# One weighted sum of squares for two norms, and one block from the feed-forward's output to the second projection

## The chip, the cores and the metric

The kernel runs on one core of a Trainium2 chip. A core has a matrix engine (TensorE, PE in the profile), two elementwise engines (VectorE, DVE; ScalarE, ACT), a slower general one (GpSimd, POOL) and SyncE (SP), which here only issues DMAs. The engines run side by side and wait for each other by semaphores. The metric is the device time of one launch in microseconds (us); lower is better.

## The reference, cut to what matters

The program is two transformer blocks over 256 tokens of width 1024, in float32. The place of the change is the end of the first block and the beginning of the second:

```python
# end of the first block
    hn = rms_norm(h, norm_ffn)
    gate_ffn, up_ffn = jnp.split(hn @ w_ffn_in, [FFN_HIDDEN], axis=-1)
    h = h + (jax.nn.silu(gate_ffn) * up_ffn) @ w_ffn_out
    x = rms_norm(h, norm_final)                  # the stream of the second block
# begin of the second block
    ada = silu(c) @ w_ada + b_ada                # gives shift and scale vectors
    xn = rms_norm_2(x, norm1_w) * (1 + scale) + shift
    proj = xn @ w_in                             # 4104 columns: qkv, gates, and beta and decay (8 columns)
    ...                                          # x itself is needed again for the residual
```

`rms_norm(x, g)` is `x * rsqrt(mean(x*x) + 1e-6) * g`. The feed-forward's hidden width is 2816. The three `ada` lines are written here in short; only the two vectors matter.

## The kernel before, in words

The activations lie transposed: 1024 channels are 8 groups (`KD`) of 128 partitions, and 256 tokens (`T2`) run along the free dimension. Every matrix product is done as three fast matmuls: an operand is split into a high part (an ACT copy to the matmul's format, "hi") and the rest (a DVE subtraction, "lo"), and hi·hi, hi·lo and lo·hi are added up in PSUM. So each weight tile costs an ACT copy and a DVE subtraction before PE can use it; three buffers of each (`CUT`) let that run ahead. A few small products are done with plain float32 operands; the profile shows each such matmul as two rows. Weights come by SP's DMA queue into a ring of three slots of 2 MB (`load_slots`, L221).

The stretch in question is a chain of program blocks. A block ends with all engines meeting.

1. **The feed-forward's block** (from L1587). PE makes 22 pairs of gate and up tiles (L1595). The norm before it is applied late: DVE scales the gate by `frs` (L1647), ACT takes the sigmoid (L1630), DVE multiplies gate and sigmoid (L1651) and then by up (L1653); the factor that is still missing is put on the output. Then 11 pieces of output weights (L1610) add into 8 PSUM banks. In each piece the two hidden groups are taken one after the other over all 8 banks. At the end DVE scales each bank by `frs2` (L1663) and adds it to the stream `hT` (L1665).
2. **`rms_norm`** (L236 to L261): squares on DVE and ACT, 8 float32 matmuls with a matrix of ones to sum them (L248), a square root on ACT (L254), a reciprocal (L259) and 8 scalings on DVE (L261). It is the first block's final norm.
3. **A block** in which ACT copies the normed stream to `xT` (L1680) and DVE and ACT compute a few columns of gains and bounds (L1687 to L1709).
4. **`rms_norm` again**, now the second block's first norm, with a shift added by ACT (L269).
5. **A block** with one GpSimd memset (L1723).
6. **`project`** (L294) for the second projection, with 32 tiles of 128 columns. ACT and DVE first split the activations as a whole and three weight tiles (L332, L351). Then PE does one tile after the other (24 matmuls each, L385), ACT and DVE empty the banks in turn (L1728, L1729), split the weights three tiles ahead, and do in hooks (`front_pe`, `front_act`, `front_dve`) what the finished tiles allow: the short convolution (L1829, L1832), its activation (L1803, L1837), squares and their sums (L1840, L1778). After tile 1 PE also makes the 8 columns of beta and decay with 16 float32 matmuls (L1769). DVE makes 4 copies at tile 30 (L1862).

Nothing here is scheduled by a tool. The order on every engine is the order in which the code is written.

## Time and profile before

| | us |
|---|---|
| median of 3 runs (lowest to highest) | 1763.94 (1761.31 to 1767.03) |
| the profiled execution, whole | 1757.34 |
| its span, first to last instruction | 1755.6 |
| PE busy in the span | 1536.9 (88%) |
| DVE busy | 1009.0 (57%) |
| ACT busy | 675.2 (38%) |
| POOL busy | 140.3 (8%) |

The page gives busy time per engine, 40 slices of the span, and the costliest groups of instructions by source line. The finer views are the timeline (one row for an instruction or for several alike, with its start, its duration, and in brackets how long the engine had been idle and who released it) and the table by stretches (busy time of every engine in given windows and the clock granted to PE, where 1.00 is 2.4 GHz and 0.50 is 1.2 GHz). PE's matmuls overlap: one is shown as 0.28 us long, but at full clock one starts every 0.12 us.

### The profile page before, as it was taken

Reading aid. Unit: us, or ns where it says so; the run is one execution under the profiler, and the core shown is the slowest. Engines: PE = TensorE matmul, PEld = TensorE weight load, DVE = VectorE, ACT = ScalarE, POOL = GpSimd, SP = SyncE. Lnnn points to the kernel's source line nnn. Section 1 sums busy time; section 2 is a strip of 40 time slices with the busy share of each in tenths; the row PEclk is TensorE's granted clock in tenths of the full one; section 3 lists DMA queues with packets and bytes.
Section 4 is the critical chain, followed back from the end, with each engine's and each line's share of the span. In section 5 each row is a group of like instructions: output and inputs, shape, how many; then the busy total and the mean of one; then the engine's idle time right before and its main releaser. Section 6 shows DMA issues by size and latency. Waiting matters only on the chain. (4 is left out here: it accounts for less than half of the span.)

```text
span 1755.6 us, 29260 instructions
## 1 busy us (share of the span) xinstructions
PE 1536.9 (88%) x11916; PEld 1278.5 (73%) x11916; DVE 1009.0 (57%) x1501; ACT 675.2 (38%) x910; POOL 140.3 (8%) x238
## 2 busy tenths in 40 slices
PE   7987697999999679976466679999999999999996
PEld 6975485999999659946456677777777777777774
DVE  5546565486664448544484555656566665566653
ACT  4342324455443244511413433444444444444441
POOL 7000000000000000000040020000000000000000
PEclk9976798999999889979687789999999999999998
DMA  7422300545554517350050386988988899988880
GB/s 250 156 96 88 106 4 1 192 155 188 190 190 142 122 48 155 134 192 1 26 167 1 119 303 250 346 331 323 344 320 337 330 335 333 341 333 337 333 314 24
DMA packets 113221, 349.27 MB, mean 199 GB/s; under 512 B 9633, under 2 KB 33392, under 8 KB 96448
## 3 DMA queue, kind: packets, MB, share of 16 engines
q1 hardware_dynamic: 103184, 315.75, 50.3%
q0 software_dynamic: 8240, 27.40, 5.2%
q10 hardware_dynamic: 1664, 4.26, 0.7%
q8 instruction: 94, 1.54, 0.4%
q14 instruction: 39, 0.32, 0.1%
HBM read 345.15 MB, written 2.23 MB: 198 GB/s over the span
## 5 line engine op out<-in xcount | busy, mean ns | idle before, releaser
L2830 DVE TENSOR_TENSOR weights_lo<-raw_weights,weights_hi 128x2048 fp32r<-128x2048 f32 x99 | 223.8, 2288 | 82.7 <-ACT weights_hi L2734 82.7
L2734 ACT ACTIVATE weights_hi<-raw_weights 128x2048 fp32r<-128x2048 f32 x99 | 185.4, 1910 | 23.4 <-DMA raw_weights<-in_w_gate 20.0
L2536 PE MATMUL bank<-x_hi,weights_hi 128*128 128x256 f32 x544 | 154.8, 285 | 0.0
L2537 PE MATMUL bank<-x_lo,weights_hi 128*128 128x256 f32 x544 | 154.6, 284 | 0.0
L2538 PE MATMUL bank<-x_hi,weights_lo 128*128 128x256 f32 x544 | 154.6, 284 | 0.0
L385 PE MATMUL bank<-in_x_hi,in_w_hi 128*128 128x256 f32 (+2 forms) x472 | 139.3, 295 | 15.9 <-DVE in_w_lo L351 15.9
L385 PE MATMUL bank<-in_x_hi,in_w_lo 128*128 128x256 f32 (+2 forms) x472 | 137.3, 291 | 0.0
L385 PE MATMUL bank<-in_x_lo,in_w_hi 128*128 128x256 f32 (+2 forms) x472 | 137.2, 291 | 0.0
L2616 PE MATMUL bank<-raw_weights,gathered_pair 128*64 128x512 f32 x512 | 113.4, 595 | 0.0
L2536 PEld LDWEIGHTS bank<-x_hi,weights_hi 128*128 128x128 f32 x544 | 105.1, 193 | 2.3 <-issue 1.6
L1508 DVE TENSOR_TENSOR ffn_weights_lo<-weight_ring,ffn_weights_hi 128x2048 fp32r<-128x2048 f32 x33 | 75.6, 2293 | 54.0 <-ACT ffn_weights_hi L1503 54.0
L2537 PEld LDWEIGHTS bank<-x_lo,weights_hi 128*128 128x128 f32 x544 | 105.2, 193 | 0.7
L2538 PEld LDWEIGHTS bank<-x_hi,weights_lo 128*128 128x128 f32 x544 | 105.1, 193 | 0.0
L351 DVE TENSOR_TENSOR in_w_lo<-weight_ring,in_w_hi 128x1024 fp32r<-128x1024 f32 (+1 forms) x59 | 71.5, 1217 | 58.5 <-ACT in_w_hi L332 58.5
L385 PEld LDWEIGHTS bank<-in_x_hi,in_w_hi 128*128 128x128 f32 (+1 forms) x472 | 91.8, 194 | 17.8 <-DVE in_w_lo L351 16.4
L1595 PE MATMUL bank<-merge_x_hi,ffn_weights_hi 128*128 128x256 f32 x352 | 99.3, 282 | 2.6 <-PEq L319 2.6
L1595 PE MATMUL bank<-merge_x_lo,ffn_weights_hi 128*128 128x256 f32 x352 | 99.1, 281 | 0.0
L1595 PE MATMUL bank<-merge_x_hi,ffn_weights_lo 128*128 128x256 f32 x352 | 99.0, 281 | 0.0
L385 PEld LDWEIGHTS bank<-in_x_lo,in_w_hi 128*128 128x128 f32 (+1 forms) x472 | 91.9, 195 | 0.3
L385 PEld LDWEIGHTS bank<-in_x_hi,in_w_lo 128*128 128x128 f32 (+1 forms) x472 | 91.7, 194 | 0.1
L385 PE MATMUL bank<-merge_x_hi,merge_w_hi 128*128 128x256 f32 x256 | 73.8, 288 | 11.7 <-DVE merge_w_lo L351 9.8
L2616 PEld LDWEIGHTS bank<-raw_weights,gathered_pair 128*64 128x64 f32 x512 | 35.3, 137 | 66.6 <-issue 66.6
(579 smaller groups left out, 3749.3 us busy)
## 6 DMA issues: line engine op xcount, KB each, us to landing
raw_weights<-in_w_gate SPq DMA_DIRECT2D x64, 1024.0 KB, 8.8
raw_weights<-in_w_up SPq DMA_DIRECT2D x64, 1024.0 KB, 9.0
raw_weights<-in_w_down SPq DMA_DIRECT2D x64, 1024.0 KB, 8.4
weight_ring<-in_w_in SPq DMA_DIRECT2D x17, 2048.0 KB, 9.1
mixer_memory<-in_w_ada SPq DMA_DIRECT2D x96, 256.0 KB, 3.8
weight_ring<-in_w_ffn_in SPq DMA_DIRECT2D x22, 1024.0 KB, 6.7
weight_ring<-in_w_ffn_out SPq DMA_DIRECT2D x5, 2048.0 KB, 7.9
weight_ring<-in_w_out SPq DMA_DIRECT2D x4, 2048.0 KB, 7.7
```

The source lines that it names most:

```text
L351: s_tlo.on(V.tensor_tensor(lo, src, hi.bitcast(F32), ALU.subtract))
L385: mm = T.matmul(bank[m % banks][0:w, 0:n], weights[:, k, :], x[:, r0 + k, :], start=(k == 0 and weights is hi and x is x_hi), stop=(k == r ...
L1508: s_rest.on(V.tensor_tensor(as_piece(f_lo[r % CUT], r), src, as_piece(f_hi[r % CUT], r).bitcast(F32), ALU.subtract))
L1595: mm = T.matmul(bank[2 * (m % 4) + up][:, 0:T2], w[:, k, up, :], x[:, k, :], start=(k == 0 and w is hi and x is fx_hi), stop=(k == KD - 1 ...
L2536: T.matmul(out_, hi[:, d, cut], x_hi[:, d, :], start=(d == 0), stop=False)
L2537: T.matmul(out_, hi[:, d, cut], x_lo[:, d, :], start=False, stop=False)
L2538: mm = T.matmul(out_, lo[:, d, cut], x_hi[:, d, :], start=False, stop=(d == KD - 1))
L2616: mm = T.matmul(bank[4][lanes, :].rearrange("p (a b) -> p a b", b=FE), xp[:, d, lanes], raw_w[:, r:r + 2, d * FE:d * FE + FE], start=(d == ...
L2734: S.activation(w_hi[:, n % 4, :], raw_w[:, k % RAW, :], ACT.Copy).then_inc(s_hi.sem, 1)
L2830: V.tensor_tensor(w_lo[:, n % 4, :], raw_w[:, k % RAW, :], w_hi[:, n % 4, :].bitcast(F32), ALU.subtract).then_inc(s_lo.sem, 1)
```

## The change

- The two norms become one. With g the final norm's gain, the product of both inverse norms is 1 / sqrt(mean(h² (g² + eps)) + eps²). So one sum of h² weighted by (g² + eps) is enough, and the second block's input is made from `hT` directly. ACT squares with the square root of the weight as scale; GpSimd adds 5 of the 7 further squares into the first (named `second_squares`), the last two go to PE separately: 3 float32 matmuls with ones in place of 8.
- In the feed-forward, up is normed as well (one more DVE operation per pair, `fup`), so that the output needs no scaling: one DVE add per bank in place of a multiplication and an add.
- The last piece of output weights goes bank by bank (both hidden groups of a bank in a row), so that each bank is finished 6 matmuls after the one before.
- The whole stretch from the feed-forward to the end of the projection is one block. The projection's first three weight tiles are split ahead of the norm's work. Its activations are split group by group as they are made (ACT makes hi with the shift, DVE makes lo from the same source), and PE takes tiles 0 and 1 together, group by group.
- The 8 columns of beta and decay use split operands: 48 fast matmuls in place of 16 float32 ones.
- The stream itself (the final norm's output, for the residual) is normed during the projection: 8 ACT squares at tiles 8 to 11, 7 GpSimd adds, one float32 matmul at tile 16, a logarithm and an exponential on ACT at tiles 20 and 25, 8 DVE scalings at tiles 29 and 30. The few columns of gains and bounds move to tiles 19 and 26. `xT` is now a view of `hT`, and its copy is gone.
- Tensors are placed at offsets written out, so that what used to be freed and taken anew can overlap in time.

The core of the diff:

```diff
 def project(..., weights_first=False, together=1):
+                    if together > 1:
+                        source = tiles[0][3]
+                        group = [operands(("w", m)) for m in range(together)]
+                        pe.wait_ge(s_tlo.sem, split_at["w", together - 1])
+                        for k in range(KD):
+                            pe.wait_ge(late[source].sem, late[source].count(k + 1))
+                            for m, (_, hi, lo) in enumerate(group):
+                                for weights, x in ((hi, x_hi), (hi, x_lo), (lo, x_hi)):
+                                    mm = T.matmul(bank[m][...], weights[:, k, :], x[:, k, :], ...)
...
 # feed-forward, DVE, pair m
-                    s_hid.on(V.tensor_tensor(fprod, bank[b], fsig, ALU.mult))
-                    s_hid.on(V.tensor_tensor(fprod, fprod, bank[b + 1], ALU.mult))
+                s_up_n.on(V.tensor_tensor(fup, bank[b + 1], frs, ALU.mult))
+                s_hid.on(V.tensor_tensor(fprod, fgate, fsig, ALU.mult))
+                s_hid.on(V.tensor_tensor(fprod, fprod, fup, ALU.mult))
...
-                for m in range(KD):
-                    s_out_n.on(V.tensor_tensor(fout[:, m % 2, :], bank[m][:, 0:T2], frs2, ALU.mult))
-                    dve_s.on(V.tensor_tensor(hT[:, m, N_META:T1], hT[:, m, N_META:T1], fout[:, m % 2, :], ALU.add))
-        rms_norm(hT[:, :, N_META:T1], x_new, lambda j: param("norm_final", j), None, ...)
-                act_s.on(S.activation(xT, x_new, ACT.Copy))
-        rms_norm(xT, hm, lambda j: gain1[:, j:j + 1], lambda j: mod[:, j:j + 1], ...)
+        def second_norm_dve(dve):
+            for m in range(KD):
+                dve.wait_ge(s_out_m.sem, s_out_m.count(m + 1))
+                s_added.on(V.tensor_tensor(xT[:, m, :], xT[:, m, :], bank[m][:, 0:T2], ALU.add))
+            dve.wait_ge(s_root2.sem, s_root2.count(1))
+            s_root2.on(V.reciprocal(rs_in, rs_in))
+            for m in range(KD + 1):
+                if m < KD:
+                    s_t2.on(V.scalar_tensor_tensor(out=ht[:, m, :], in0=xT[:, m, :], scalar=gain_in[:, m:m + 1], in1=rs_in, ...))
+                if m:
+                    dve.wait_ge(s_x2hi.sem, s_x2hi.count(m))
+                    s_x2lo.on(V.scalar_tensor_tensor(out=x2_lo[:, m - 1, :], in0=ht[:, m - 1, :], scalar=mod[:, m - 1:m], ...))
+        def second_norm_act(act):
+            for m in range(KD):
+                act.wait_ge(s_added.sem, s_added.count(m + 1))
+                s_sq2.on(S.activation(squares2[:, m, :], xT[:, m, :], ACT.Square, scale=gain_root[:, m:m + 1]))
+            act.wait_ge(s_sum2.sem, s_sum2.count(1))
+            s_root2.on(S.activation(rs_in, bank[0][:, 0:T2], ACT.Sqrt, bias=eps_in, scale=1.0 / D))
+            for m in range(KD):
+                act.wait_ge(s_t2.sem, s_t2.count(m + 1))
+                s_x2hi.on(S.activation(x2_hi[:, m, :], ht[:, m, :], ACT.Identity, bias=mod[:, m:m + 1]))
```

The order of instructions shows it at two places. First PE, from the last output matmuls of the feed-forward (bank 7) to the first of the projection. Before:

```order
L1610 MATMUL bank6<-ffn_hidden_hi,ffn_weights_lo2 128x256
L1610 MATMUL bank7<-ffn_hidden_hi,ffn_weights_hi2 128x256
L1610 MATMUL bank7<-ffn_hidden_lo,ffn_weights_hi2 128x256
L1610 MATMUL bank7<-ffn_hidden_hi,ffn_weights_lo2 128x256
L1576 UNCONDITIONAL_BRANCH
L243 UNCONDITIONAL_BRANCH
L248 MATMUL bank0<-mixer2_kept,kept 128x256 x8
L230 UNCONDITIONAL_BRANCH
L243 UNCONDITIONAL_BRANCH
L248 MATMUL bank0<-mixer2_kept,kept 128x256 x8
L230 UNCONDITIONAL_BRANCH
L372 UNCONDITIONAL_BRANCH
```

And in the changed kernel (the numbers behind names only number the tensors):

```order
L1682 MATMUL bank7<-ffn_hidden_hi_5168,ffn_weights_lo2_3842 128x256
L1690 MATMUL bank0<-second_squares_5179,kept 128x256
L1693 MATMUL bank0<-second_squares_5179,kept 128x256 x2
L381 UNCONDITIONAL_BRANCH
L391 MATMUL bank0<-in2_x_hi_5177,in2_w_hi0_5171 128x256
L391 MATMUL bank0<-in2_x_lo_5178,in2_w_hi0_5171 128x256
L391 MATMUL bank0<-in2_x_hi_5177,in2_w_lo0_5174 128x256
L391 MATMUL bank1<-in2_x_hi_5177,in2_w_hi1_5172 128x256
L391 MATMUL bank1<-in2_x_lo_5178,in2_w_hi1_5172 128x256
L391 MATMUL bank1<-in2_x_hi_5177,in2_w_lo1_5175 128x256
```

Sixteen summing matmuls have become three, the meetings of all engines between them are gone (one branch is left), and banks 0 and 1 take turns by group of channels. The second place is DVE between the feed-forward's last bank and the projection's tiles. Before:

```order
L1663 TENSOR_TENSOR ffn_memory<-bank7,ffn_memory 128x256
L1665 TENSOR_TENSOR kept<-kept,ffn_memory 128x256
...
L236 TENSOR_TENSOR mixer2_kept<-kept 128x256 x4
L256 UNCONDITIONAL_BRANCH
L259 RECIPROCAL mixer2_kept<-mixer2_kept 128x256
L261 SCALAR_TENSOR_TENSOR mixer2_kept<-kept,mixer2_kept 128x256 x8
...
L1709 TENSOR_SCALAR kept<-kept 128x4
...
L351 TENSOR_TENSOR in2_x_lo<-mixer2_kept,in2_x_hi 128x2048
L351 TENSOR_TENSOR in2_w_lo0<-weight_ring,in2_w_hi0 128x1024
```

In the changed kernel:

```order
L360 TENSOR_TENSOR in2_w_lo2_5176<-weight_ring,in2_w_hi2_5173 128x1024
L1761 SCALAR_TENSOR_TENSOR kept<-kept 128x8
...
L1773 TENSOR_TENSOR kept<-kept,bank0 128x256
...
L1773 TENSOR_TENSOR kept<-kept,bank7 128x256
L1775 RECIPROCAL ffn_memory_3845<-ffn_memory_3845 128x256
L1779 SCALAR_TENSOR_TENSOR mixer2_kept_5170<-kept,ffn_memory_3845 128x256 x2
L1783 SCALAR_TENSOR_TENSOR in2_x_lo_5178<-mixer2_kept_5170,kept,in2_x_hi_5177 128x256
L1779 SCALAR_TENSOR_TENSOR mixer2_kept_5170<-kept,ffn_memory_3845 128x256
...
L360 TENSOR_TENSOR in2_w_lo0_5174<-weight_ring,in2_w_hi0_5171 128x1024
L1805 COPY mixer2_kept_5170<-bank1 128x256
```

The three weight splits stand ahead of the stream's adds now, one reciprocal is left of two, and scaling and splitting alternate group by group.

## Rows read from the trace of the kernel before

**Rows 1.** Timeline, PE: last output matmul to the third projection tile.
```profile
593.73 0.28 PE L1610 MATMUL bank<-ffn_hidden_hi,ffn_weights_lo 128*128 128x256 f32 x1
598.78 5.13 PE L248 MATMUL bank<-mixer_kept,kept 128*128 128x256 f32 x16 [4.76 <-DVE mixer_kept L236]
614.84 5.63 PE L248 MATMUL bank<-mixer_kept,kept 128*128 128x256 f32 x16 [10.93 <-DVE mixer_kept L236]
632.78 0.58 PE L385 MATMUL bank<-in_x_hi,in_w_hi 128*128 128x256 f32 x1 [12.31 <-DVE in_w_lo L351]
640.04 7.07 PE L1769 MATMUL bank<-mixer_kept,kept 128*4 128x256 f32 x32
647.04 0.39 PE L385 MATMUL bank<-in_x_hi,in_w_hi 128*128 128x256 f32 x1
```

**Rows 2.** Timeline, DVE: the same stretch.
```profile
591.53 0.43 DVE L1663 TENSOR_TENSOR ffn_memory<-bank,ffn_memory 128x256 f32<-128x256 f32 x1 [10.46 <-PE bank L1610]
...
597.55 0.43 DVE L1665 TENSOR_TENSOR kept<-kept,ffn_memory 128x256 f32<-128x256 f32 x1
...
604.46 1.75 DVE L259 RECIPROCAL mixer_kept<-mixer_kept 128x256 f32<-128x256 f32 x1 [4.73 <-ACT mixer_kept L254]
606.24 3.26 DVE L261 SCALAR_TENSOR_TENSOR mixer_kept<-kept,mixer_kept 128x256 f32<-128x256 f32 x8
...
631.51 3.49 DVE L351 TENSOR_TENSOR in_w_lo<-weight_ring,in_w_hi 128x1024 fp32r<-128x1024 f32 x3
```

**Rows 3.** Timeline, ACT: the same stretch.
```profile
603.95 0.47 ACT L254 ACTIVATE mixer_kept<-bank,kept 128x256 f32<-128x256 f32 x1 [3.04 <-PE bank L248]
...
623.33 3.30 ACT L269 ACTIVATE mixer_kept<-mixer_kept,kept 128x256 f32<-128x256 f32 x8 [2.34 <-DVE mixer_kept L261]
```

**Rows 4.** Windows of 2 us: busy time per engine (count), then PEclk, DMA, GB/s.
```profile
596.00:598.00 2.00, 0.00 (x0) 0.00 (x0) 1.91 (x5) 0.00 (x0) 0.00 (x0) 1.00 0.00 0
598.00:600.00 2.00, 1.22 (x3) 1.05 (x4) 1.43 (x4) 1.71 (x5) 0.00 (x0) 0.56 0.00 0
...
634.00:636.00 2.00, 2.00 (x11) 2.00 (x11) 1.00 (x1) 0.00 (x0) 0.00 (x0) 0.55 0.00 0
636.00:638.00 2.00, 2.00 (x19) 2.00 (x18) 0.00 (x0) 0.73 (x2) 0.00 (x0) 1.00 0.00 0
```

**Rows 5.** Timeline, POOL, DVE, ACT: adding squares ahead of the feed-forward.
```profile
391.73 1.07 POOL L1554 TENSOR_TENSOR ffn_memory<-ffn_memory 128x256 f32<-128x256 f32 x1 [1.81 <-ACT ffn_memory L1533]
397.05 0.74 POOL L1554 TENSOR_TENSOR ffn_memory<-ffn_memory 128x256 f32<-128x256 f32 x1 [4.24 <-ACT ffn_memory L1533]
...
392.13 0.96 DVE L1544 SCALAR_TENSOR_TENSOR merge_x_lo<-kept,merge_x_hi 128x256 fp32r<-128x256 f32 x1
...
397.10 0.41 DVE L1519 TENSOR_TENSOR kept<-kept,bank 128x256 f32<-128x256 f32 x1
398.09 0.48 DVE L1544 SCALAR_TENSOR_TENSOR merge_x_lo<-kept,merge_x_hi 128x256 fp32r<-128x256 f32 x1 [0.58 <-ACT merge_x_hi L1532]
...
396.57 0.40 ACT L1533 ACTIVATE ffn_memory<-kept 128x256 f32<-128x256 f32 x1
```

**Rows 6.** Groups by line and shape, PE, 15 to 120 us: a narrow weight tile.
```profile
L385 PE MATMUL bank<-in_x_hi,in_w_hi 128*128 128x272 f32 x208 | 61.7, 296 | 3.6 <-DVE in_w_lo L351 3.6
...
L385 PE MATMUL bank<-in_x_hi,in_w_hi 128*32 128x272 f32 x8 | 2.3, 287 | 0.0
```

**Rows 7.** Timeline, DVE: a late pair of the feed-forward's input.
```profile
522.29 0.42 DVE L1651 TENSOR_TENSOR ffn_memory<-bank,ffn_memory 128x256 f32<-128x256 f32 x1 [0.49 <-ACT ffn_memory L1630]
```

**Rows 8.** Who waited for whom, 632 to 745 us: total, times, longest.
```profile
ACT mixer_kept L1728 <- PE bank L385: 41.6, 11, 11.3
...
PE bank L1778 <- DVE mixer_kept L1840: 2.1, 2, 1.1
```

**Rows 9.** Timeline, DVE: the projection's last tiles.
```profile
742.21 2.48 DVE L1862 COPY mixer_memory<-bank 128x512 f32<-128x512 f32 x4
747.61 0.42 DVE L1729 COPY mixer_kept<-bank 128x256 f32<-128x256 f32 x1 [2.93 <-PE bank L385]
```

More of the change, by code:

```diff
@@ L146, in build @@
         row_sel = mem.take(GH, P)
+        AT_SMALL = mem.at
         small = mem.take(256)
@@ L373, in _ @@
                 def _(pe):
+                    if together > 1:
[6 more added lines that the diff above has]
+                                for weights, x in ((hi, x_hi), (hi, x_lo), (lo, x_hi)):
+                                    mm = T.matmul(bank[m][0:tiles[m][2], 0:n], weights[:, k, :], x[:, k, :],
+                                                  start=(k == 0 and weights is hi and x is x_hi), stop=(k == KD - 1 and weights is lo))
+                                if k == KD - 1:
+                                    pe_s.on(mm)
+                        if "pe" in between:
+                            for m in range(together):
+                                between["pe"](pe, m)
                     for m, (s, c0, w, source) in enumerate(tiles):
+                        if together > 1 and m < together:
+                            continue
                         pe.wait_ge(s_tlo.sem, max(split_at["w", m], split_at.get(("x", source), 0)))
@@ new lines, in _ @@
+        @block.scalar
+        def _(act):
+            for r in range(1, CUT):
+                cut_piece(act, r)
+            act.wait_ge(s_hsum.sem, s_hsum.count(1))
+            s_hlog.on(S.activation(flog, bank[7][:, 0:T2], ACT.Ln, bias=eps_rms, scale=1.0 / D))
+            act.wait_ge(s_hlog.sem, s_hlog.count(1))
+            s_hrs.on(S.activation(frs, flog, ACT.Exp, scale=-0.5))
+            for m in range(n_in):
+                act.wait_ge(s_gate_n.sem, s_gate_n.count(m + 1))
+                if m >= 2:
+                    act.wait_ge(s_hid.sem, s_hid.count(2 * (m - 1)))
+                s_sig.on(S.activation(fsig[:, m % 2, :], fgate[:, m % 2, :], ACT.Sigmoid))
+                cut_piece(act, m + CUT)
+                act.wait_ge(s_hid.sem, s_hid.count(2 * m + 2))
+                s_fhi.on(S.activation(ffn_hi[m], fprod[:, m % 2, :], ACT.Copy))
+            for r in range(n_in + CUT, n_in + n_out):
+                cut_piece(act, r)
@@ L1766, in front_pe @@
             if m == 1:
+                pe.wait_ge(s_bahi.sem, s_bahi.count(2))
                 for i in range(2):
                     for k in range(KD):
[L1769 to L1770 removed]
+                        for w, x in ((ba_hi, x2_hi), (ba_hi, x2_lo), (ba_lo, x2_hi)):
+                            mm = T.matmul(bank[4][0:GH, i * T2:i * T2 + T2], w[:, k, GH * i:GH * i + GH], x[:, k, :],
+                                          start=(k == 0 and w is ba_hi and x is x2_hi), stop=(k == KD - 1 and w is ba_lo))
                 s_ba.on(mm)
@@ L1779, in front_pe @@
                 s_ssq.on(mm)
+            if m == 16:
+                pe.wait_ge(s_stracc.sem, s_stracc.count(KD - 1))
+                s_strn.on(T.matmul(bank[5][:, 0:T2], ones, ht[:, 0, :], start=True, stop=True))
             if m == 28:
+                pe.wait_ge(s_strn.sem, s_strn.count(2))
                 pe.wait_ge(s_row_dve.sem, 4)
@@ L1865, in front_dve @@
                 dve_s.on(V.tensor_copy(cols, bank[6][:, 0:4 * GH].rearrange("p (a b) -> p a b", b=GH)))
-        with ExitStack() as stack:
-            project([hm], T2, [(W_IN2 + m // 4, (m % 4) * P, P, 0) for m in range(32)], put_in2, W_IN2, 8,
-                    split_memory(stack, "in2_", KD, T2), banks=4, between={"pe": front_pe, "act": front_act, "dve": front_dve})
-        MIX2B = total - SECOND - MIX2 - 32
-        m2b = Memory(mixer_stack.enter_context(nc.sbuf_tensor("mixer2_late", [P, MIX2B], F32)), 0, MIX2B)
+        project([None], T2, [(W_IN2 + m // 4, (m % 4) * P, P, 0) for m in range(32)], put_in2, W_IN2, 8,
+                (x2_hi, x2_lo, w2_hi, w2_lo), banks=4, late={0: s_x2lo}, block=block, together=2,
+                between={"pe": front_pe, "act": front_act, "dve": front_dve,
+                         "act_first": second_norm_act, "dve_first": second_norm_dve})
+        ffn_stack.close()
+        MIX2B = AT_MIX2 - AT_PARTS2
+        m2b = Memory(place("mixer2_late", [P, MIX2B], AT_PARTS2, F32), 0, MIX2B)
         Dm = m2b.take(2 * GH, P)
```

371 lines of the change are left out of this document (214 added, 157 removed).

## The prediction, on record before the result was known

> **What bounds the kernel here.** I read the timeline of PE first. Its last feed-forward matmul starts at 593.73 us, and the first matmul of the projection starts at 632.78: 39.1 us apart, in which PE only runs two groups of summing matmuls, 5.13 and 5.63 us [rows 1]. Everything else in that stretch is a chain through DVE and ACT in which one engine works and the others wait. The timeline of DVE gives its links: per bank a multiplication and an add until 597.98, squares, one reciprocal of 1.75 us, eight scalings in 3.26 us, and then the same again for the second norm, and at the end the split of the activations and of three weight tiles (the latter 3.49 us) [rows 2]. ACT has a root of 0.47 us and eight shifts in 3.30 us in it [rows 3]. The table by stretches then shows what the holes do to PE's clock: still 1.00 at 596 to 598, 0.56 at 598 to 600 after 4.76 us without work, and when the projection starts at 632.78 it runs at half speed until about 636 [rows 1, 4]. At half clock a matmul starts every 0.21 us, at full every 0.12.
>
> Behind 632.78 PE is the bound. ACT waits 41.6 us for PE's tiles, and PE waits only for two sums, 2.1 us in total [rows 8]. So work taken from the gap is gained in full, and work that moves into the projection is free as long as DVE and ACT still keep ahead.
>
> **The forecast, step by step.** I compare the moment at which PE starts projection tile 2: 647.04 before [rows 1]. Handovers from one engine to the next are the gaps of rows 1 to 3, about 0.05. All times are on the trace of before, since nothing ahead of 593.73 should move.
>
> 1. *Up to the last bank.* The number of output matmuls is the same, so bank 7 is done at about 594.05. Banks now come every 6 × 0.12 = 0.72 us, and a DVE add takes 0.43 [rows 2] and an ACT square 0.40 [rows 5], so both keep up. The last square is ready at 594.05 + 0.43 + 0.40 and two handovers of some 0.05, about 595.0.
> 2. *The sum.* GpSimd has 5 adds. One took 0.74 us where DVE only did adds from PSUM, and 1.07 beside DVE work on two SBUF inputs [rows 5]. The first can start when the second square is ready, six banks earlier, 595.0 − 4.3 = 590.7. At 0.80 with its handover the fifth ends at 594.7, at 1.13 it ends at 596.4. I take the first, since DVE's adds in this stretch read one input from PSUM. Then three float32 matmuls: 8 of them took 5.13 us partly at half clock [rows 1], so 0.43 each at full clock and up to 0.85 at half. Two can run before the last square comes. The sum is there at about 596.0 (bounds: 595.8 and 596.4 + 2.6 = 599.0).
> 3. *The one inverse norm.* Root 0.47 [rows 3], reciprocal 1.75 [rows 2], handovers 0.1: 598.3.
> 4. *The first group.* Scaling 0.48, shift and round on ACT 0.5, lo on DVE 0.48, handovers 0.1: 1.6 us, so PE starts at 599.9. The weight splits (3.49 us [rows 2]) and the small columns are done earlier, while PE works on the last pieces.
> 5. *Tiles 0 and 1.* DVE needs two operations per group, 2 × 3.26/8 = 0.82 us, so the eighth lo is ready 7 × 0.82 = 5.7 us after the first, at 605.6. PE needs 6 × 0.12 = 0.72 per group at full clock and 1.28 at half. With the half clock lasting as at the projection's start before, some 3 us [rows 1, 4], PE does 2.3 groups by 602.9 and the other 5.7 in 4.1 us: 607.0. If DVE alone sets the end it is 606.3; if the half clock lasts 5 us, 608.1. I take 607.3.
> 6. *Beta and decay.* Before 7.07 us for 16 float32 matmuls [rows 1], 0.22 per row of the trace. Now 48 fast ones. If they start every 0.12 like other fast matmuls they take 5.8. A fast matmul with a tile of only 32 columns had 287 ns where the full one had 296 [rows 6], so few columns cost nothing extra there. If 4 columns ran at the float32 pace they would take 48 × 0.22 = 10.6. I take 5.8, so tile 2 starts at 613.1.
>
> That is 647.04 − 613.1 = 33.9 us earlier. Against it stand:
>
> 7. *PE in the projection.* One more float32 sum at tile 16: +0.5.
> 8. *The end of the projection.* Eight scalings of 0.41 (3.3 us) stand ahead of or between DVE's last copies. The copies before ran from 742.21 to 744.69, and DVE then waited 2.93 us for the last tile [rows 9]. 3.3 against a wait of 2.9: +0.4.
> 9. *ACT and DVE in the projection.* ACT gains 8 × 0.40 + 0.5 + 0.5 + 0.2 = 4.4 us, DVE seven tiny operations of some 0.17. The 41.6 us for which ACT waits for PE [rows 8] cover that. GpSimd's adds run beside DVE work with two SBUF inputs, where a DVE operation of 0.48 took 0.96 [rows 5]. Just after tile 9 PE waits for DVE's squares, 1.1 us [rows 8], so there a slower DVE shows. I take +0.5, bounds 0 and 3.4 (seven adds of 0.48).
> 10. *The feed-forward's pairs.* One more DVE operation of 0.42 in each of 22. It falls into the 0.49 us in which DVE waits for the sigmoid [rows 7], so it costs nothing. Without that cover it would delay the hidden tile by 0.4, which only the last pair shows, as PE is bound there. If DVE were the bound it would cost 22 × 0.42 = 9.2. The exponential that is no longer made saves 0.4 on ACT off the path: 0.
>
> Sum: −33.9 + 0.5 + 0.4 + 0.5 = −32.5 us. On the profiled execution of 1757.34 that gives 1724.8. The median of the runs shown is 1763.94, 6.6 us above that execution, and the changed kernel will be timed like the median: 1763.9 − 32.5 = 1731.4 us.
>
> **A rule of the skill against the trace.** GpSimd's add took 0.74 us beside a DVE add that reads PSUM and 1.07 beside a DVE operation on two SBUF inputs, and that DVE operation took 0.96 in place of 0.48 [rows 5]. The Trainium skill, page "SBUF — State Buffer", section "Who interferes with whom", says why: a DVE instruction with two SBUF inputs contends with a GpSimd instruction that reads SBUF, one of the two waits until the other has ended, and a DVE instruction with one SBUF input doesn't take part. By that rule step 2 stands as I took it. It speaks against step 9: a DVE instruction that comes second is held for up to a whole add, so by the rule the seven adds could cost 7 × 0.74 = 5.2 us if all of them stood on the path, where the row's 0.48 each makes 3.4.
>
> **Rivals.**
>
> - *A, the sum comes late.* GpSimd's adds run at 1.13 and the three matmuls at half clock: the sum at 599.0, 3.0 later, and tiles 0 and 1 end at 611 with a slow clock. Then −28.5, 1735.4. For it: both durations occur before, and the longer one is the rule beside weight splits [rows 5]. Against: no weight split is near here.
> - *B, the projection pays back.* If ACT's 4.4, DVE's 3.3 + 1.2 and PE's 0.5 all came on the path, 9.4 us would go: −24.5, 1739.4. For it: the three-tile lead of the weight splits goes through both engines. Against: PE's waits in that stage are 2.1 us [rows 8]. A milder form, 3 us more, is likelier.
> - *C, the 4-column matmuls run at the float32 pace:* 10.6 in place of 5.8, −27.7, 1736.2. Against it rows 6.
> - *D, the feed-forward becomes DVE-bound:* +9.2, −23.3, 1740.6. Against it the idle time ahead of the same operation [rows 7].
> - *E, slower than before: PE stays at 1.2 GHz through the projection,* because its operands now trickle in. The tiles 2 to 31 are 720 matmuls, each (0.21 − 0.12) = 0.09 us longer: +65, so +32 in total, 1796. It decides from 361 slow matmuls on, 15 tiles. Against: at half clock PE needs 1.28 per group where DVE needs 0.82, so PE is without holes, and in the same state before it was back at full clock after some 3 us [rows 4].
> - *F, the gap doesn't shrink,* because something still keeps PE from starting, a weight slot for instance: no change. The projection's first slot becomes free with the eighth of the eleven pieces of output weights, three pieces before the end, so I see nothing for it.
>
> **How the numbers follow.** The forecast with its small variations has 0.62, A 0.14, B 0.08, C 0.06, D 0.04, E 0.02, F 0.02, and 0.02 for anything else. The range has the mechanism's bounds (−34.4 with the clock up and nothing paid back in step 9, −26 for A or C with part of B) and about 3 us for the level of the runs, whose lowest and highest are 5.7 apart: 1725 to 1741. It leaves out D's end, E and F. A change under 0.3%, 5.3 us, can't be told from none with this kernel. All cases but E and F are beyond it on the fast side: faster 0.95, same 0.02, slower 0.03.
>
> **What would show it.** In the changed kernel's timeline PE's last output matmul still starts at about 593.7; three float32 matmuls end by 596.0 (step 2; 599 is A); one root, one reciprocal; the first projection matmul at about 600 (step 4), the 48 narrow ones at about 607.3 in 5.8 us (steps 5 and 6; 10.6 is C), and tile 2 at about 613. From there to the end of the projection, before 747.6 + 0.4 − 647.0 = 101, it should be 102.4 (steps 7 to 9; 106 or more is B). The feed-forward's start to its end stays as long (D). A granted clock of 0.50 far behind 605 would be E. The forecast fails if tile 2 starts after 618 or if more than 4 us are lost behind it.

## The result, and the profile after

The changed kernel took 1717.26 us in the median (1712.75 to 1727.64, 4 runs) against 1765.16 (1761.31 to 1767.03, 4 runs): a ratio of 0.974, 95% interval 0.969 to 0.979. That is 14 us below the forecast and outside its range. Two later comparisons of the same two kernels gave 0.980 (0.977 to 0.984) and 0.980 (0.976 to 0.984); their medians lie 36.1 and 32.5 us apart. The profiled execution took 1718.13 us, 1716.4 of it span, with a mean granted clock of 0.932 (before 0.924).

The timeline of PE over the same stretch (start, us, engine, line, tiles, count, idle time before and its releaser), to be read against [rows 1]:

```profile
592.00 0.28 PE L1682 MATMUL bank<-ffn_hidden_hi,ffn_weights_lo 128*128 128x256 f32 x1
593.49 0.67 PE L1690 MATMUL bank<-second_squares,kept 128*128 128x256 f32 x2 [1.21 <-POOL second_squares L1750]
594.00 1.03 PE L1693 MATMUL bank<-second_squares,kept 128*128 128x256 f32 x4
599.05 0.55 PE L391 MATMUL bank<-in_x_hi,in_w_hi 128*128 128x256 f32 x1 [4.03 <-DVE in_x_lo L1783]
...
607.01 0.28 PE L1846 MATMUL bank<-in_x_hi,beta_gate_w_hi 128*4 128x256 f32 x1
...
612.47 0.28 PE L411 MATMUL bank<-in_x_hi,in_w_hi 128*128 128x256 f32 x1
```

From the last output matmul to the first of the projection there are 7.05 us, before 39.05, and to tile 2 20.47 us, before 53.31. The 48 narrow matmuls take 5.46 us, one every 0.11; the stretch that they stand for took 7.00 before. The chain between them in the timelines of POOL, ACT and DVE, against [rows 2, 3]:

```profile
589.10 4.25 POOL L1750 TENSOR_TENSOR second_squares<-second_squares 128x256 f32<-128x256 f32 x5 [189.20 <-ACT second_squares L1793]
```

```profile
592.78 0.51 ACT L1793 ACTIVATE second_squares<-kept 128x256 f32<-128x256 f32 x1 [0.20 <-DVE kept L1773]
595.06 0.47 ACT L1796 ACTIVATE ffn_memory<-bank,kept 128x256 f32<-128x256 f32 x1 [1.78 <-PE bank L1693]
```

```profile
592.32 0.42 DVE L1773 TENSOR_TENSOR kept<-kept,bank 128x256 f32<-128x256 f32 x1 [0.29 <-PE bank L1682]
595.57 1.75 DVE L1775 RECIPROCAL ffn_memory<-ffn_memory 128x256 f32<-128x256 f32 x1 [2.83 <-ACT ffn_memory L1796]
597.36 0.88 DVE L1779 SCALAR_TENSOR_TENSOR mixer_kept<-kept,ffn_memory 128x256 f32<-128x256 f32 x2
598.42 0.49 DVE L1783 SCALAR_TENSOR_TENSOR in_x_lo<-mixer_kept,kept,in_x_hi 128x256 fp32r<-128x256 f32 x1 [0.18 <-ACT in_x_hi L1799]
...
603.84 0.48 DVE L1783 SCALAR_TENSOR_TENSOR in_x_lo<-mixer_kept,kept,in_x_hi 128x256 fp32r<-128x256 f32 x1 [0.18 <-ACT in_x_hi L1799]
...
706.91 3.25 DVE L1955 SCALAR_TENSOR_TENSOR kept<-kept,mixer_kept 128x256 f32<-128x256 f32 x8
710.07 2.48 DVE L1978 COPY mixer_memory<-bank 128x512 f32<-128x512 f32 x4
712.46 0.42 DVE L1805 COPY mixer_kept<-bank 128x256 f32<-128x256 f32 x1
```

GpSimd's row of 4.25 us is five adds of 0.73, each starting 0.88 behind the one before. One reciprocal is left, and lo is ready group by group, every 0.79 us. The last three rows answer to [rows 9]: the eight scalings of the stream stand ahead of the copies, and DVE now runs into the last tile without the wait of 2.93. The stretches of 2 us (busy us and count of PE, PEld, DVE, ACT, POOL, then the granted clock), against [rows 4]:

```profile
592.00:594.00 2.00, 0.79 (x6) 0.56 (x4) 0.45 (x2) 1.02 (x2) 1.28 (x3) 1.00 0.34 101
...
596.00:598.00 2.00, 0.00 (x0) 0.00 (x0) 1.96 (x3) 0.12 (x1) 0.00 (x0) 0.77 0.01 4
598.00:600.00 2.00, 0.95 (x4) 0.98 (x5) 1.82 (x5) 1.29 (x3) 0.00 (x0) 0.50 0.00 0
600.00:602.00 2.00, 2.00 (x12) 2.00 (x11) 2.00 (x7) 1.30 (x3) 0.00 (x0) 0.50 0.00 0
602.00:604.00 2.00, 2.00 (x11) 2.00 (x11) 1.82 (x6) 1.24 (x3) 0.00 (x0) 0.53 0.00 0
604.00:606.00 2.00, 2.00 (x19) 2.00 (x18) 0.32 (x1) 0.00 (x0) 0.00 (x0) 1.00 0.00 0
```

The sums run at full clock. In the wait of 4.03 us behind them the clock falls to half (1.2 GHz), and it is back (2.4 GHz) at about 604, 4.9 us after the projection has started. The table of waits for 612 to 713 us, against [rows 8], and a pair of the feed-forward in DVE's timeline, against [rows 7]:

```profile
ACT mixer_kept L1804 <- PE bank L411: 31.6, 10, 9.8
...
PE bank L1855 <- DVE mixer_kept L1935: 2.6, 2, 1.7
```

```profile
520.65 0.42 DVE L1728 TENSOR_TENSOR ffn_memory<-bank,ffn_memory 128x256 f32<-128x256 f32 x1
521.22 0.43 DVE L1733 TENSOR_TENSOR ffn_memory<-ffn_memory 128x256 f32<-128x256 f32 x1 [0.15 <-ACT ffn_memory L1708]
```

ACT still waits 31.6 us for PE and PE 2.6 us for sums: PE stays the bound. In [rows 8] these are 41.6 and 2.1, but that stretch begins with the first projection matmul; from tile 2 on ACT's wait was 36.4 before. The 0.5 that PE waits longer is one wait, and its cause is shown under e5. The added multiplication (L1728) lies where DVE waited 0.49 for the sigmoid; 0.15 of that wait is left. From its first matmul to its last the feed-forward takes 192.0 and 191.8 us in the first two traces of after (194.1 in a third), 192.7 and 191.8 before. So the trace shows the change at work as forecast, and what is to be explained is a time lower than forecast. From the start of tile 2 to the copy of the last tile (L1805 at 712.46) there are 99.99 us, before 100.57.

### The profile page after: what moved, and what is told of

It reads as the page before. It is cut to its first block and busy times, and to the rows that moved or that the text cites. A ratio compares the mean times of both kernels' runs of the same rounds, so it can differ in the third digit from the quotient of the medians.

```text
span 1716.4 us, 29256 instructions
## 1 busy us (share of the span) xinstructions
PE 1518.9 (88%) x11908; PEld 1265.3 (74%) x11908; DVE 1012.0 (59%) x1516; ACT 672.7 (39%) x916; POOL 150.8 (9%) x251
## 5 line engine op out<-in xcount | busy, mean ns | idle before, releaser
L411 PE MATMUL bank<-in_x_hi,in_w_hi 128*128 128x256 f32 (+2 forms) x456 | 133.3, 292 | 3.6 <-DVE in_w_lo L360 3.6
L411 PE MATMUL bank<-in_x_hi,in_w_lo 128*128 128x256 f32 (+2 forms) x456 | 131.8, 289 | 0.0
L411 PE MATMUL bank<-in_x_lo,in_w_hi 128*128 128x256 f32 (+2 forms) x456 | 131.5, 288 | 0.0
L1665 PE MATMUL bank<-merge_x_hi,ffn_weights_hi 128*128 128x256 f32 x352 | 99.3, 282 | 2.6 <-PEq L328 2.6
L411 PEld LDWEIGHTS bank<-in_x_hi,in_w_hi 128*128 128x128 f32 (+1 forms) x456 | 87.6, 192 | 4.4 <-DVE in_w_lo L360 3.7
L411 PEld LDWEIGHTS bank<-in_x_lo,in_w_hi 128*128 128x128 f32 (+1 forms) x456 | 87.5, 192 | 0.3
L411 PEld LDWEIGHTS bank<-in_x_hi,in_w_lo 128*128 128x128 f32 (+1 forms) x456 | 87.5, 192 | 0.1
```

The lines of the kernel that those rows point to most:

```text
L411: mm = T.matmul(bank[m % banks][0:w, 0:n], weights[:, k, :], x[:, r0 + k, :], start=(k == 0 and weights is hi and x is x_hi), stop=(k == r ...
L1665: mm = T.matmul(bank[2 * (m % 4) + up][:, 0:T2], w[:, k, up, :], x[:, k, :], start=(k == 0 and w is hi and x is fx_hi), stop=(k == KD - 1 ...
```

## The experiments

Four kernels ran on one chip, four on a second and three on a third, on each beside runs of the kernel before. For each I give the time, and from its trace two marks: the distance from the last output matmul to tile 2 ("gap", 53.31 before and 20.47 after in the first traces), and from tile 2 to the small copy that follows 0.33 behind the last tile's ("projection", 100.9 and 100.3).

**Both kernels again (e1, e2, e9).** No edit.

> The kernel before, unchanged, profiled and timed again. Its first profiled execution took 1757.3 us and the runs beside it 1761 to 1767. Theory V (the part of the result beyond the gap is run variation, carried by PE's clock): the profiled execution is above 1757, 1762 to 1767, at a granted clock below 0.924, and the extra time is spread over stages that the change doesn't touch. Rival L (the levels are right and the change itself gains more than its gap): again 1757, and the times of the repetition agree with the first within 0.1%.

> The changed kernel, unchanged, profiled and timed again. Theory V: the time beside the kernel before comes nearer to the 35 us that the profile shows up to the end of the projection than the first comparison did: a ratio of 0.976 to 0.981, and the repetitions spread over 8 us or more, the shorter ones with the higher clock. Rival L: ratio 0.974 or below again.

> The changed kernel, unchanged, a third time, as the reference for the next kernel on the same chip. Theory V (the first comparison's 0.974 was the level of a few runs): ratio to before between 0.978 and 0.982. From the last feed-forward matmul to projection tile 2 again 20.5 us; from there to the last small copy 98.9, 100.3 or 101.9 us, according to the granted clock of its last 20 us (1.00, 0.92 or 0.84).

Measured: before again 1755.55 (12 runs, 1748.52 to 1762.53), ratio to the 23 runs of before beside it 0.998 (0.996 to 1.001). After again 1721.87 (5 runs, 1718.18 to 1723.40), 0.980; the third time 1726.73 (6 runs, 1715.96 to 1732.72), 0.980. The gap was 54.23 for before and 20.69 and 19.76 for after; the projection 100.9 for before, 100.2 and 100.3 for after. What the traces show is thus steady within 1 us, while the times of one kernel spread over 1%. The third gap of after is the shorter one because the half clock lasts only 3.3 us of the projection there, in place of 4.9. All 43 runs of before in the three later comparisons have a median of 1758.1 (1749.9 to 1768.5), with e1's 12 added 1758.0; the 11 later runs of after have one of 1723.4 (1716.0 to 1732.7): 34.7 us apart. With the first four runs of each, 47 against 15, it is 1759.0 against 1721.9. The three runs from which I had taken 1763.94 lie in the upper part of that spread. It goes with the mean granted clock: 0.914 to 0.929 in the 43 runs, 9.8 us less for each 0.01 more (correlation −0.68); 0.926 to 0.937 in the 15, 14.5 us for each 0.01 (−0.76). Which of the two brings the other isn't shown.

Not all that I had expected came. The profiled execution of e1 took 1758.37 at a clock of 0.926, not 1762 to 1767 below 0.924, and the runs of e2 spread over 5.2 us, not 8. Rival L fares worse: its ratio of 0.974 or below didn't come back in either comparison, and the median of e1 is 8 us below the 1764 of the first runs. So the level of the first few runs is the likelier account. Why just those came out so far apart no run here shows.

**The feed-forward's part alone (e3).** Before, with up normed in the pairs, the last piece bank by bank, one add per bank:

```diff
-                s_out_n.on(V.tensor_tensor(fout[:, m % 2, :], bank[m][:, 0:T2], frs2, ALU.mult))
-                dve_s.on(V.tensor_tensor(hT[:, m, N_META:T1], hT[:, m, N_META:T1], fout[:, m % 2, :], ALU.add))
+                dve_s.on(V.tensor_tensor(hT[:, m, N_META:T1], hT[:, m, N_META:T1], bank[m][:, 0:T2], ALU.add))
```

> The kernel before with the feed-forward part of the change alone: up is normed too, the output is no longer scaled, the last piece goes bank by bank. Both norms, their blocks and the projection stay as before. By the steps of the prediction: DVE's last add ends 0.43 + 0.4 us behind the last bank in place of 4.1 us behind it, so 3.3 to 3.5 us are gained, 1761.7 where before has 1765. If the added DVE operation were not hidden (rival D) the pairs cost up to 9 us and it is 3 to 6 us slower than before.

Measured: 1752.70 (12 runs), ratio 0.997 (0.995 to 1.000): 5.3 us below the median of before, and the interval reaches from 0.5 to 9.5 us. Its timeline of PE:

```profile
593.84 0.28 PE L1612 MATMUL bank<-ffn_hidden_hi,ffn_weights_lo 128*128 128x256 f32 x1
595.37 3.72 PE L248 MATMUL bank<-mixer_kept,kept 128*128 128x256 f32 x16 [1.26 <-DVE mixer_kept L236]
610.02 6.30 PE L248 MATMUL bank<-mixer_kept,kept 128*128 128x256 f32 x16 [10.93 <-DVE mixer_kept L236]
628.63 0.58 PE L385 MATMUL bank<-in_x_hi,in_w_hi 128*128 128x256 f32 x1 [12.31 <-DVE in_w_lo L351]
```

The first sum starts 1.53 us behind the last output matmul (5.05 in [rows 1]), so PE's clock hasn't fallen when it comes and the eight matmuls take 3.72 in place of 5.13. The second sum takes 0.67 more than before. The gap is 49.35: 4.0 us of the 33 are this part (4.9 against the second trace of before), where 3.3 to 3.5 had been expected. Rival D, 3 to 6 us slower, is out.

**The projection in a block of its own (e4).** After, but the norm's work is one block and the projection another, so that the weight splits come behind the meeting; tiles 0 and 1 stay together:

```diff
+        block.scalar(second_norm_act)
+        block.vector(second_norm_dve)
-        project(..., banks=4, late={0: s_x2lo}, block=block, together=2, ...)
+        project(..., banks=4, late={0: s_x2lo}, together=2, ...)
...
```

> The changed kernel with the projection in a block of its own again: the norm's work ends, the engines meet, then the first three weight tiles are split and PE begins, still with tiles 0 and 1 together. Theory (the gap bounds, every us in it counts): PE starts about 604.3 + 0.8 for the meeting + 1.0 for the first ACT copy + 2.5 for two DVE rests = 608.6 in place of 599.0, and tile 2 at about 621 in place of 612.4: 8 to 9.5 us slower than the changed kernel. Rival: the meeting and the splits run beside the other engines' work, and it is less than 3 us slower.

Measured: 1731.26 (6 runs), 0.987 (0.983 to 0.991), 9.4 us above after's 1721.87 on the same chip, where 8 to 9.5 had been expected. In its timelines of PE and DVE:

```profile
610.46 0.58 PE L391 MATMUL bank<-in_x_hi,in_w_hi 128*128 128x256 f32 x1 [13.09 <-DVE in_w_lo L360]
```

```profile
606.18 0.48 DVE L1785 SCALAR_TENSOR_TENSOR in_x_lo<-mixer_kept,kept,in_x_hi 128x256 fp32r<-128x256 f32 x1 [0.18 <-ACT in_x_hi L1801]
608.05 3.50 DVE L360 TENSOR_TENSOR in_w_lo<-weight_ring,in_w_hi 128x1024 fp32r<-128x1024 f32 x3 [1.39 <-ACT in_w_hi L341]
```

PE now waits for the weights, whose splits start after all eight groups are split. Its gap is 30.11: the common block with the early weight splits is worth 9.6 us (9.4 to 10.4 against after's three traces), 9.1 of them up to PE's first projection matmul.

**Two norms in a row (e7).** After, with the two norms computed one behind the other in the common block, in the same way as the one (5 GpSimd adds, 3 matmuls, root, reciprocal); the stream's norm then isn't needed in the projection and is left out there:

```diff
+            for m in range(KD):
+                s_added.on(V.scalar_tensor_tensor(out=xT[:, m, :], in0=xT[:, m, :], scalar=param("norm_final", m), in1=rs_in, ...))
...
+            s_root2.on(V.reciprocal(rs_in, rs_in))
...
-                s_sq2.on(S.activation(squares2[:, m, :], xT[:, m, :], ACT.Square, scale=gain_root[:, m:m + 1]))
+                s_sq2.on(S.activation(squares2[:, m, :], xT[:, m, :], ACT.Square))
```

> The changed kernel with two norms one after the other in the same block, as the reference has them: sum, root, reciprocal, scaling of the stream, then squares, sum, root, reciprocal again; the stream's own norm is then not needed in the projection and is left out there. Theory (each us in the chain counts): the second round costs 8 scalings 3.3, square 0.5, GpSimd's lag about 1.2, three sums 1.0, root 0.5, reciprocal 1.75, handovers 0.3: PE's first projection matmul comes 8 to 9 us later, and with the projection about 1 us shorter the kernel is 7 to 8 us slower than the changed one. Rival (merging the norms is the main part of the gain): 15 us or more.

Measured: 1731.28 (5 runs), 0.985 (0.983 to 0.987). Its timelines of DVE and PE:

```profile
602.03 5.14 DVE L1781 SCALAR_TENSOR_TENSOR kept<-kept,ffn_memory 128x256 f32<-128x256 f32 x8
611.28 1.75 DVE L1784 RECIPROCAL ffn_memory<-ffn_memory 128x256 f32<-128x256 f32 x1 [4.11 <-ACT ffn_memory L1810]
```

```profile
607.80 1.22 PE L1697 MATMUL bank<-second_squares,kept 128*128 128x256 f32 x2 [8.11 <-POOL second_squares L1758]
608.82 1.91 PE L1700 MATMUL bank<-second_squares,kept 128*128 128x256 f32 x4
614.76 0.55 PE L391 MATMUL bank<-in_x_hi,in_w_hi 128*128 128x256 f32 x1 [4.02 <-DVE in_x_lo L1792]
```

The gap is 30.74, so merging the norms takes 10.3 us off it (10.1 to 11.0 against after's three traces). PE's first projection matmul comes 18.00 us behind the last output matmul, 11.0 later than in after, where 8 to 9 had been expected. Two links of the second norm run slower than in [rows 1, 2]: the eight scalings take 5.14 beside GpSimd's adds where they took 3.26, and the three matmuls, behind a wait of 8.11 us, take 2.9 at half clock where the first three take 1.5 in after.

**The stream's norm left out (e5).** The squares, adds, sum, logarithm, exponential and scalings of tiles 8 to 30 are left out; the scalings:

```diff
...
-            if m in (29, 30):
-                for j in range(4 * (m - 29), 4 * (m - 29) + 4):
-                    V.scalar_tensor_tensor(out=xT[:, j, :], in0=xT[:, j, :], scalar=param("norm_final", j), in1=ht[:, 1, :], ...)
```

> The changed kernel without the final norm of the stream: the 8 squares, GpSimd's 7 adds, the one sum, the logarithm and exponential and the 8 scalings in the projection are left out (the residual is the unnormed stream). Prediction's steps 7 to 9: these cost 1.4 us. Read in the profile as the time from projection tile 2 to the last small copy, 100.3 us in the changed kernel: 99.3 to 98.9. Rival B (the projection pays back): 97 or less. In the total it can't be told from the changed kernel.

Measured: 1724.65 (5 runs), 0.981 (0.979 to 0.982): no gain over after that the times could show. Its projection took 100.9 us, longer than after's 100.3, where 98.9 to 99.3 had been expected. The granted clock goes with that: behind the first 80 us from tile 2 its mean is 0.84 there and 0.92 in after. In all kernels the clock is 1.00 in those first 80 us and can fall when the 16 products with 4 rows come. Sorted by the clock of the rest: at 0.84 the projection takes 100.8 to 100.9 without the stream's norm (before twice, e3, e5) and 101.7 to 102.0 with it (e6, e8); at 0.91 or 0.92 it takes 99.3 without (e7) and 100.2 to 100.3 with it (after three times); at 1.00 it takes 98.9 with it (e4, e11). So the stream's norm costs 1.0 us and the fall of the clock some 3.

Half of that 1.0 is one wait. PE's second pair of sums, and what DVE and GpSimd do ahead of it, first in after, then in e5, which has no GpSimd adds there:

```profile
639.38 1.13 PE L1855 MATMUL bank<-mixer_kept,kept 128*128 128x256 f32 x4 [1.67 <-DVE mixer_kept L1935]
637.38 1.22 DVE L1932 TENSOR_TENSOR mixer_memory<-mixer_memory,mixer_kept 128x512 f32<-128x512 f32 x1
636.90 1.16 POOL L1757 TENSOR_TENSOR mixer_kept<-mixer_kept 128x256 f32<-128x256 f32 x1 [43.48 <-ACT mixer_kept L1889]
```

```profile
645.00 1.13 PE L1850 MATMUL bank<-mixer_kept,kept 128*128 128x256 f32 x4 [1.13 <-DVE mixer_kept L1916]
643.53 0.68 DVE L1913 TENSOR_TENSOR mixer_memory<-mixer_memory,mixer_kept 128x512 f32<-128x512 f32 x1
```

GpSimd's first add lies over DVE's multiplication of two SBUF inputs; that takes 1.22 in place of 0.68, and PE waits 1.67 in place of 1.13 (0.68 and 1.13 in e7 too, which has no such adds either). The rest, some 0.4, is PE's own float32 sum at tile 16.

**Tiles 0 and 1 one after the other (e6).**

```diff
-                ..., block=block, together=2,
+                ..., block=block,
```

> The changed kernel with projection tiles 0 and 1 one after the other; tile 0 still takes its groups as they come. Theory: tile 0 ends with the last group, about 604.9 (3 matmuls behind it), tile 1 takes 2.9 us more, 607.8, against 607.0 with both together: 0.8 us slower, since the half clock makes the pair wait less for DVE. Rival: if DVE alone sets the pair's end, taking them together is worth a whole tile less three matmuls, 2.5 us.

Measured: 1726.67 (5 runs), 0.982 (0.980 to 0.984), gap 22.01: tile 2 comes 1.3 to 2.3 us later than in after's three traces. Not all of it is the order of the tiles: the half clock covers 6.8 us of the projection in e6, 4.9 in the first trace of after and 6.0 in e11. Tiles 0 and 1 take 9.49 us in e6 and 8.44 in e11, so taking them together is worth some 1 us, near the 0.8 expected. In the times the difference to after can't be told.

**Fewer adds on GpSimd, and PE kept busy (e8, e11).** 3 adds on GpSimd and 5 matmuls in the sum in both; e8 also puts 26 matmuls whose result nobody reads into PE's wait:

```diff
-            pe.wait_ge(s_acc2.sem, s_acc2.count(KD - 3))
+            pe.wait_ge(s_acc2.sem, s_acc2.count(3))
-            for m in range(KD - 2, KD):
+            for m in range(4, KD):
...
+            for i in range(26):
+                T.matmul(bank[7][:, 0:T2], w2_hi[2][:, 0, :], ffn_hi[FT - 1], start=True, stop=True)
...
-            for j in range(1, KD - 2):
+            for j in range(1, 4):
```

> Meant to be faster than both: the changed kernel with 3 GpSimd adds in place of 5 (PE sums 5 operands), and with 26 extra matmuls into an unused bank between the sum and the first projection tile, whose result nobody reads. Theory (the wait for GpSimd, 1.2 us, and the half clock until about 604 are what is left in the gap): the sum ends 1.0 us earlier, the granted clock stays 1.00 from 594 to 604, and DVE then sets the pair's end: tile 2 comes 2.5 to 3.0 us earlier than 20.5 us behind the last feed-forward matmul. Rival: extra work doesn't hold the clock, and only 1 us is gained.

> The changed kernel with 3 GpSimd adds in place of 5 and 5 operands summed by PE, without the extra matmuls of e8_warm. Theory: PE no longer waits 1.2 us for GpSimd, the first projection matmul comes about 6.1 us behind the last feed-forward matmul in place of 7.05, and tile 2 at 19.5 in place of 20.5, at half clock until the middle of the pair. Rival: the wait for GpSimd was hidden behind the last square, and nothing moves.

Measured: e8 1719.59 (5 runs), 0.979 (0.978 to 0.981); e11 one run of 1729.48. The timelines of PE, first e8, then e11:

```profile
592.56 0.28 PE L1682 MATMUL bank<-ffn_hidden_hi,ffn_weights_lo 128*128 128x256 f32 x1
592.68 0.59 PE L1690 MATMUL bank<-second_squares,kept 128*128 128x256 f32 x2
593.11 1.89 PE L1693 MATMUL bank<-second_squares,kept 128*128 128x256 f32 x8
594.65 3.43 PE L1697 MATMUL bank<-ffn_hidden_hi,in_w_hi 128*128 128x256 f32 x26
599.03 0.36 PE L391 MATMUL bank<-in_x_hi,in_w_hi 128*128 128x256 f32 x1 [0.95 <-DVE in_x_lo L1786]
```

```profile
600.75 1.89 PE L1693 MATMUL bank<-second_squares,kept 128*128 128x256 f32 x8
606.67 0.55 PE L391 MATMUL bank<-in_x_hi,in_w_hi 128*128 128x256 f32 x1 [4.02 <-DVE in_x_lo L1783]
```

With 3 adds PE doesn't wait for GpSimd any more and the projection starts 6.47 us behind the last output matmul, 0.6 earlier; 0.9 to 1.0 had been expected. Of that little reaches tile 2: the gap is 20.37 in e11, where 19.5 had been expected and after has 20.47, 20.69 and 19.76. Its tiles 0 and 1 take 8.44 us (after 7.96), since they start earlier and the half clock covers more of them, 6.0 us in place of 4.9. In e8 the first projection matmul takes 0.36 where it took 0.55: the clock stays up, and the gap is 18.12, 2.3 less than in e11. Of that its projection loses 1.4 again against after's 100.3, since there the clock fell further at the end (0.84). In the times e8 can't be told from after (0.979 against 0.980).

**PE kept busy at the end of the projection too (e10).** e8, and a matmul of 128 rows ahead of every second of the 16 products with 4 rows:

```diff
+                pe.wait_ge(dve_s.sem, dve_in2 + 13)
...
+                        T.matmul(bank[1][:, 0:T2], x2_lo[:, 0, 0:P], x2_hi[:, 0, :], start=True, stop=True)
```

> The kernel e8_warm with 8 more matmuls whose result nobody reads, one ahead of each of the 8 products that spread the decay and beta rows (only 4 of PE's rows are used by those). Theory (the clock falls in that stretch because those products hardly occupy PE, and for how long depends on where it falls in each run): the granted clock of the projection's last 20 us is 1.00, and the stretch from tile 2 to the last small copy takes 98.9 + 8 × 0.12 = 99.8 us, against 101.7 in e8_warm. Rival: the clock falls for another reason and stays at 0.84 to 0.92, and the stretch takes 102 us or more. Together with the filled gap it should then be 3 to 4 us faster than the changed kernel in the profile, which the total can hardly show.

Measured: 1728.69 (6 runs), 0.983 (0.980 to 0.986), and the projection took 106.9 us, 5 more than in e8, where I had expected less. The timeline of PE and the stretches around the products:

```profile
706.94 0.39 PE L1871 MATMUL bank<-in_x_hi,in_x_lo 128*128 128x256 f32 x1
707.25 0.69 PE L1872 MATMUL bank<-mixer_memory,kept 4*128 4x256 f32 x2
707.88 0.58 PE L1871 MATMUL bank<-in_x_hi,in_x_lo 128*128 128x256 f32 x1
708.39 1.22 PE L1872 MATMUL bank<-mixer_memory,kept 4*128 4x256 f32 x2
```

```profile
704.00:706.00 2.00, 2.00 (x11) 1.07 (x9) 2.00 (x3) 1.33 (x2) 0.00 (x0) 1.00 0.00 0
706.00:708.00 2.00, 2.00 (x8) 1.08 (x7) 2.00 (x3) 0.00 (x0) 0.00 (x0) 0.96 0.00 0
708.00:714.00 6.00, 6.00 (x12) 3.02 (x12) 0.65 (x1) 0.00 (x0) 0.00 (x0) 0.50 0.00 0
714.00:718.00 4.00, 4.00 (x18) 3.48 (x17) 0.00 (x0) 0.00 (x0) 0.00 (x0) 0.50 0.00 0
```

A group of one large matmul and two products takes 0.94 us at full clock, far above 0.12 + 2 × 0.23 (0.23 is the 3.72 us of the 16 products in e11, divided). So the stretch grew from 4.2 us in e8 to 10.3, the clock fell in it all the same, and stayed at half until 718. My idea that a few large matmuls hold the clock there is refuted in this form. In e11 the same 16 products, without any addition, ran at 1.00 throughout; in e8 and in after the clock fell in or behind them. Why it falls in one execution and not in another is open.

## Why the prediction was wrong

Its mechanism held, step by step, counted from the last output matmul:

- *Step 1.* Last square forecast at +1.3, measured +1.29: ACT's square takes 0.51, not 0.40, and the handovers are shorter.
- *Step 2.* Sum forecast at +2.3, measured +3.03. GpSimd's chain ended at +1.35, 0.4 late: an add took 0.73, as in [rows 5], but the next starts 0.88 after it, so that a handover is 0.15 and not 0.06, and the first add started 0.1 late. The three matmuls then took 1.54 with 0.14 ahead of them, in place of 3 × 0.43. The sentence that two of them can run before the last square doesn't fit: the one on GpSimd's sum is first in PE's order, the two others stand behind it, and the 596.0 itself has all three in a row behind GpSimd's 594.7. The delay is a quarter of rival A's 3 us. e11 removes the wait.
- *Steps 3 and 4.* From the sum to PE's start 3.9 forecast, 4.02 measured.
- *Step 5.* 7.4 us forecast, 7.96 measured: the half clock lasted 4.9 us, not 3. In the third trace of after it lasted 3.3, and the two tiles took 7.27.
- *Step 6.* 5.8 forecast, 5.46 measured. Rival C is out. Tile 2 comes 32.8 us earlier in the pair of first traces, 33.5 in the second; forecast 33.9.
- *Steps 7 to 9.* +1.4 forecast from tile 2 on, −0.6 measured. The work moved there costs 1.0 at equal clock: 0.54 is PE's longer wait behind GpSimd's first add, which is step 9's +0.5 (rows under e5), some 0.4 the float32 sum of step 7, and at most 0.1 DVE's scalings, where step 8 had 0.4. Rival B is out. The other 1.6 came back because the clock fell for a shorter time behind the 4-row products. I don't credit the change with it: before, e1 and e3 had 0.84 and after's three traces 0.92, but between tile 2 and the end e6, e8, e4 and e11 run the same code as after, and they had 0.84, 0.84, 1.00 and 1.00. With so few traces that isn't proven. In e7 eight DVE scalings with two SBUF inputs took 5.14 us beside GpSimd's adds and 3.26 without them [rows 2]. The Trainium skill, page "SBUF — State Buffer", section "Who interferes with whom", says that a DVE instruction with two SBUF inputs contends with a GpSimd instruction that reads SBUF; the traces of after and e7 agree. Of the up to 5.2 us that the prediction worked out by that rule for seven adds on the path, 0.54 reached it, at one of them.
- *Step 10.* Held: the feed-forward took as long as before, 192.0 us against 192.7. Rivals D, E and F are out by the same traces.

That makes −32.8 − 0.6 = −33.4 us against a forecast of −32.5. That it comes so near is partly luck: the gap closed 1.1 us less than forecast, and the clock at the end of the projection gave 1.6. (The fast bound of the range is −34.0 by its own steps, not −34.4, which changes nothing here.)

The step that failed is the last: "the changed kernel will be timed like the median". The 14.1 us between 1731.4 and 1717.26 are made up of three parts, by the medians of the three later comparisons. 5.8 are the level of before: 1763.94 of three runs against 1758.1 of 43. 6.1 are the level of after's first four runs, 1717.26 against 1723.4 for the eleven later ones. 2.2 are the size: 34.7 between those medians against 32.5. Only the first two are levels of few runs, and they lie on opposite sides; the third is no more than the noise, since the second comparison has 36.1 between its medians and the third 32.5, just the forecast. Without the 6.6 us that this step added to the profiled execution, the forecast was 1724.8, 1.4 from the 1723.4 of the later runs. I had put "about 3 us for the level of the runs, whose lowest and highest are 5.7 apart" into the range, where 43 runs are 18.6 apart. The profiled execution of before, 1757.34, was nearer to the median of the 43 than the median of the three runs was.

The two first profiled executions lie 39.2 us apart. 33.4 of it is in the stretch from the last output matmul to the end of the projection, 1.7 ahead of it and 4.0 behind it. Behind the projection the change leaves the work as it was, and that stretch took 1007.7, 1010.0 and 1006.1 us in before, e1 and e3 and 1001.3 to 1011.4 in the ten traces of after and its variants. Ahead of the last output matmul it was 591.6 to 593.8 and 591.7 to 600.4. So 5.8 us of the difference between two single executions lie where neither kernel explains them. Whether a us or two behind the projection belong to the change is open.

How the 33 divide is shown for four parts: merging the norms 10.3 (e7), the common block with early weight splits 9.6 (e4), the feed-forward's output 4.0 to 4.9 (e3), two tiles together some 1 (e6). Each was taken out of after, or put into before, alone, so they needn't add up, and each is one trace against gaps of after that differ by 0.9 among themselves. Their sum is 25 to 26. A fifth, 1.5, can be read from the rows: the columns of beta and decay take 5.46 us in place of 7.00. That the other 5 or 6 are the meetings of the engines that are gone, the copy of the stream, the columns of gains in the chain and the split of the activations as a whole is read from [rows 2, 3] and only argued.

## What to carry to other kernels

Where the bound engine stands still behind a chain of small steps on others, the saving could be forecast from the rows to about 1 us here: count the chain from the last instruction of the bound engine, look at the order in which that engine's own instructions stand when they wait, and let work flow in groups. Work moved to where the bound engine is busy isn't free either: one GpSimd add beside the wrong DVE instruction made PE wait 0.54 us longer. The measured time is another matter: a level taken from three runs was 6 us off here, so a forecast of a difference should be stated as a difference, and its range needs the spread of many runs of identical code.

## What the hardware showed that I had not expected

- Identical code ran between 1749.9 and 1768.5 us in 43 runs, with mean granted clocks of 0.914 to 0.929. The longer runs tend to be those with less clock (correlation −0.68).
- A wait of 4.0 us on PE was followed by 4.9 us of real projection work at 1.2 GHz, in another execution of the same kernel by 3.3; with 26 matmuls in the wait and 0.95 us of it left, the clock stayed at 2.4 GHz.
- The clock also fell while the profile shows PE busy all the time, in or just behind the 16 matmuls with only 4 rows: in after its mean is 0.72 in the 2 us behind them, and in e10 it was at half for 10 us. In e4 and e11 it didn't fall.
- A matmul of 128 rows between matmuls of 4 rows made a group of three 0.5 us longer at full clock, rather than 0.12 (e10).
- 48 split matmuls with 4 columns took 5.46 us, 0.11 each, as fast as ones with 128 columns; the float32 ones had 0.22 per row.
- A square with a column of scales took ACT 0.51 us (after); without one 0.42 (e7) and 0.40 [rows 5].
- GpSimd's adds of 128x256 that wait for one another started every 0.88 us, though each took 0.73 (after).
- One DVE multiplication of two SBUF inputs took 1.22 us where a GpSimd add lay over it, 0.68 where none did (after, e5).
